# Sliding attention by pairs of heads on two token tiles, and the first pair of each feed-forward written out

## What is computed

```python
kb, vb = band(k), band(v)                      # key blocks n-1 and n
scores = einsum('bnqhgd,bnkhd->bnhgqk', qb, kb) * (Dh ** -0.5)
scores = where(valid, scores, -inf)            # causal, window of 128
m = maximum(max(scores, axis=-1), sink)
e = exp(scores - m)
denom = sum(e, axis=-1) + exp(sink - m)
out = einsum('bnhgqk,bnkhd->bnqhgd', e / denom, vb)
```

## Time and profile before

| | |
|---|---|
| median of 3 runs | 2503.91 us |
| lowest and highest | 2501.05, 2506.88 us |
| the profiled execution | 2497.86 us |
| its span in the profile | 2495.9 us |
| mean granted clock of TensorE | 0.966 |
| busy in the span | PE 94%, DVE 51%, ACT 31%, POOL 6% |

### The profile page before, as it was taken

How to read it: one execution, slowest core, us unless ns; L and a number is a source line. 1 busy time by engine, 2 the same in 40 slices (tenths; PEclk the granted TensorE clock), 3 DMA queues, 4 the chain that set the end, 5 groups by cost and what they waited for, 6 DMA issues and landing times.

```text
span 2495.9 us, 28634 instructions
## 1 busy us (share of the span) xinstructions
PE 2348.9 (94%) x11659; PEld 1887.8 (76%) x11659; DVE 1281.8 (51%) x1541; ACT 776.6 (31%) x1002; POOL 139.6 (6%) x92
## 2 busy tenths in 40 slices
PE   6999999996899999999987999999988889999998
PEld 5888888865688888787875778888766647788887
DVE  5434445647454345475567454444557763534543
ACT  3312233243233322353236321222333353312211
POOL 2000001103100100020000100000100000000000
PEclk9999999988899999999999999999999899999999
DMA  4333223210032232233320133233221300233221
GB/s 138 101 101 97 89 84 95 85 55 1 26 101 101 84 101 84 84 101 102 93 77 1 52 101 98 87 103 99 74 87 44 92 1 21 99 101 101 87 99 68
DMA packets 192321, 200.54 MB, mean 80 GB/s; under 512 B 6178, under 2 KB 187520, under 8 KB 192226
## 3 DMA queue, kind: packets, MB, share of 16 engines
q1 hardware_dynamic: 192226, 199.22, 25.2%
HBM read 191.93 MB, written 2.10 MB: 78 GB/s over the span
## 4 chain that ended last, share of the span: by engine, by line
PE 83%; DVE 11%; ACT 3%; issue 2%; DMA 1%; SPq 0%; POOL 0%; DVEq 0%; ACTq 0%
PE psum L541 81%; DVE w_lo L258 1%; PE psum L933 1%; DVE sm L1891 1%; DVE free_x L1964 1%; ACT w_hi L250 1%; DVE sm L1962 1%; ACT free_h L1094 1%; PE psum L751 1%; DVE free_x L1462 0%; DVE h_lo L1465 0%; DVE rstd L1480 0%; DVE xg_lo L1462 0%; DVE free_h L1465 0%; DVE buf_b L1462 0%
## 5 line engine op out<-in xcount | busy, mean ns | idle before, releaser
L541 PE MATMUL psum<-xg_lo,w_hi 128*128 128x512 f32 x1568 | 609.8, 391 | 4.0 <-DVE xg_lo L1462 2.7
L541 PE MATMUL psum<-xg_hi,w_hi 128*128 128x512 f32 x1520 | 595.8, 392 | 2.7 <-DVE w_lo L258 2.6
L541 PE MATMUL psum<-xg_hi,w_lo 128*128 128x512 f32 x1520 | 592.6, 390 | 0.0
L250 ACT ACTIVATE w_hi<-w_raw 128x2048 fp32r<-128x2048 f32 (+1 forms) x183 | 348.2, 1903 | 535.5 <-PE psum L541 520.9
L258 DVE TENSOR_TENSOR w_lo<-w_raw,w_hi 128x2048 fp32r<-128x2048 f32 (+1 forms) x183 | 419.1, 2290 | 179.5 <-ACT w_hi L250 179.4
L541 PE MATMUL psum<-h_hi,w_hi 128*128 128x512 f32 x1144 | 453.5, 396 | 4.8 <-DVE w_lo L258 3.0
L541 PE MATMUL psum<-h_lo,w_hi 128*128 128x512 f32 x1144 | 447.7, 391 | 0.0
L541 PE MATMUL psum<-h_hi,w_lo 128*128 128x512 f32 x1144 | 447.5, 391 | 0.0
L541 PEld LDWEIGHTS psum<-xg_lo,w_hi 128*128 128x128 f32 x1568 | 295.5, 189 | 69.7 <-issue 6.5
L541 PEld LDWEIGHTS psum<-xg_hi,w_hi 128*128 128x128 f32 x1520 | 286.3, 188 | 66.6 <-issue 5.7
L541 PEld LDWEIGHTS psum<-xg_hi,w_lo 128*128 128x128 f32 x1520 | 286.2, 188 | 60.0
(11 more groups left out here) (228 smaller groups left out, 2258.9 us busy)
## 6 DMA issues: line engine op xcount, KB each, us to landing
w_raw<-in_mlp_w SPq DMA_DIRECT2D x64, 1024.0 KB, 5.2
w_raw<-in_ffn_w_gate SPq DMA_DIRECT2D x22, 1024.0 KB, 5.3
w_raw<-in_ffn_w_up SPq DMA_DIRECT2D x22, 1024.0 KB, 5.3
w_raw<-in_ffn_w_down SPq DMA_DIRECT2D x16, 1024.0 KB, 5.0
w_raw<-in_diff_w_in SPq DMA_DIRECT2D x12, 1024.0 KB, 5.1
w_raw<-in_w_in SPq DMA_DIRECT2D x9, 1024.0 KB, 5.1
w_raw<-in_dsa_w_in SPq DMA_DIRECT2D x9, 1024.0 KB, 5.1
w_raw<-in_ffn_w_down SPq DMA_DIRECT2D x8, 768.0 KB, 4.3
```

Of the source, the lines that this page charges most:

```text
L250: e.activation(w_hi[:, c % 2, 0:n], w_raw[:, c % 2, 0:n], ACT.Copy).then_inc(sem("hi_done"), 1)
L541: return pe.matmul(out, lhsT, rhs, start=start, stop=stop)
```

## The change

**Sliding attention.** A unit `u` is now a pair of heads (t = u // 2) on two of the four token tiles (0 and 1 for even u, 2 and 3 for odd u). Each head of the pair has one of the two banks, and one product of 512 columns writes the masks of both tiles into a bank (for tiles 2 and 3 the same 256 columns are read twice). Behind both masks come the scores tile by tile, the head in the lower half of the array and the head in the upper half in turn. The values go tile by tile too, the two halves of the output partitions in turn. Transposes, their copies, the exponentials and the normalisation keep shape and count: again eight units of four tiles. Since a unit now has two heads, the sinks are read for both: VectorE keeps them negated, takes the minimum with the negated maximum, and subtracts in one more small instruction, which gives the argument of the small exponential. The wait for a free output bank stands before even units only. The mask constants change places so that 512 columns in a row serve tiles 0 and 1.

**Feed-forwards.** On ScalarE and VectorE the pair j = 0 of the first group of each feed-forward is written out ahead of the loop, which then starts at 1. In this pair ScalarE does `hi` of block c+2 ahead of its first activation; in the squared form VectorE also does `lo` of block c+2 ahead of the first evacuation. In the gated form VectorE's order stays.

```diff
@@ TensorE
-            def a1_scores(h):
-                half, kv = h % 2, h // 4
...
-                for n in range(NT):
-                    dst = bank[2 * (h % 2) + n // 2][:, (n % 2) * 256:(n % 2 + 1) * 256]
-                    mm(dst, ident_bf[:], first_mask if n == 0 else band_mask, True, False)
...
-                        last = mm(dst, q, keys[hs, (n - 1) * P:(n + 1) * P], False, True)
+            def a1_scores(u):
+                t, kv = u // 2, u // 4
+                if u >= 2:
+                    pe.wait_ge(sem("a1_exp"), u - 1)
+                for half in range(2):
+                    dst = bank[2 * (u % 2) + half]
+                    if u % 2 == 0:
+                        mm(dst, ident_bf[:], first_mask, True, False)
+                    else:
+                        mm(dst.rearrange("p (b k) -> p b k", b=2), ident_bf[:],
+                           band_mask.unsqueeze(1).to_broadcast([P, 2, 2 * P]), True, False)
+                for b in range(2):
+                    n = 2 * (u % 2) + b
+                    for half in range(2):
+                        hs = slice(HD * half, HD * half + HD)
+                        keys = ak if half == kv else ak_swap
+                        first = P if n == 0 else 0
+                        last = mm(bank[2 * (u % 2) + half][:, b * 256 + first:(b + 1) * 256],
+                                  aq[hs, t, n * P:(n + 1) * P], keys[hs, (n - 1) * P + first:(n + 1) * P], False, b == 1)
...
-                if t >= 2:
+                if t >= 2 and u % 2 == 0:
                     pe.wait_ge(sem("a1_out"), t - 1)
-                for n in range(NT):
+                for b in range(2):
+                    n = 2 * (u % 2) + b
                     for w in ((1,) if n == 0 else (0, 1)):
...
+                        for half in range(2):
+                            last = mm(bank[6 + t % 2][HD * half:HD * half + HD, n * P:(n + 1) * P],
+                                      av[:, n - 1 + w, kv * HD:(kv + 1) * HD],
+                                      a1_pt(u)[:, 4 * half + 2 * b + w, :], w == 0 or n == 0, w == 1)
@@ ScalarE
+                    def square_pair(j, first=False):
+                        if first:
+                            hi(act, c + 2, j)
+                        for s_ in range(2):
+                            act.wait_ge(sem("hmul"), 2 * j + (h0 + s_ + 1))
+                            a(hidden(p)[0][:, bass.ds(4 * j + 2 * s_, 2), :], buf_d[:], ACT.Copy).then_inc(sem("h_hi_done"), 1)
+                            if s_ or not first:
+                                hi(act, c + 2 + s_, j)
...
-                a(sm[:, so + 12:so + 16], sm[:, so + 4:so + 8], ACT.Exp,
-                  bias=sinks[:, h:h + 1]).then_inc(sem("a1_exp"), 1)
+                a(sm[:, so + 12:so + 16], sm[:, so + 12:so + 16], ACT.Exp).then_inc(sem("a1_exp"), 1)
@@ VectorE
+                    def square_pair(j, first=False):
+                        if first:
+                            lo(dve, c + 2, j)
+                        for s_ in range(2):
+                            evac_scaled(c + s_, buf_b, j)
...
+                            if s_ or not first:
+                                lo(dve, c + 2 + s_, j)
...
-                ts(sm[:, so + 4:so + 8], sm[:, so:so + 4], sinks[:, h:h + 1], -1.0, ALU.max, ALU.mult).then_inc(sem("a1_m"), 1)
+                sink = no_sinks[:, h // 2 * 2:h // 2 * 2 + 2].unsqueeze(2).to_broadcast([P, 2, 2])
+                low = sm[:, so + 4:so + 8].rearrange("p (a b) -> p a b", b=2)
+                link(stt(low, sm[:, so:so + 4].rearrange("p (a b) -> p a b", b=2), -1.0, sink, ALU.mult, ALU.min))
+                tt(sm[:, so + 12:so + 16].rearrange("p (a b) -> p a b", b=2), low, sink, ALU.subtract).then_inc(sem("a1_m"), 1)
```

More of the change, by code:

```diff
@@ L1116, in ffn, with gated_pair @@
                     hcount[0] += tiles // 2
+                    def gated_pair(j, first=False):
+                        if first:
+                            hi(act, c + 2, j)
+                        act.wait_ge(sem("evac"), 2 * j + (c + 1))
+                        a(buf_c[:], buf_a[:], ACT.Silu).then_inc(sem("silu"), 1)
+                        if not first:
+                            hi(act, c + 2, j)
+                        act.wait_ge(sem("hmul"), j + (h0 + 1))
+                        a(hidden(p)[0][:, bass.ds(2 * j, 2), :], buf_d[:], ACT.Copy).then_inc(sem("h_hi_done"), 1)
+                        hi(act, c + 3, j)
@@ new lines, in square_pair @@
+                    def square_pair(j, first=False):
+                        if first:
+                            hi(act, c + 2, j)
+                        for s_ in range(2):
[3 more added lines that the diff above has]
+                                hi(act, c + 2 + s_, j)
+                    pair, n_pairs = (gated_pair, tiles // 2) if gated else (square_pair, tiles // 4)
@@ L1117, in ffn @@
+                    if g == 0:
+                        pair(0, first=True)
                     if gated:
                         scount[0] += tiles // 2
-                        with act.Fori(0, tiles // 2) as j:
-                            act.wait_ge(sem("evac"), 2 * j + (c + 1))
-                            a(buf_c[:], buf_a[:], ACT.Silu).then_inc(sem("silu"), 1)
-                            hi(act, c + 2, j)
-                            act.wait_ge(sem("hmul"), j + (h0 + 1))
-                            a(hidden(p)[0][:, bass.ds(2 * j, 2), :], buf_d[:], ACT.Copy).then_inc(sem("h_hi_done"), 1)
-                            hi(act, c + 3, j)
-                    else:
-                        with act.Fori(0, tiles // 4) as j:
-                            for s_ in range(2):
-                                act.wait_ge(sem("hmul"), 2 * j + (h0 + s_ + 1))
-                                a(hidden(p)[0][:, bass.ds(4 * j + 2 * s_, 2), :], buf_d[:], ACT.Copy).then_inc(sem("h_hi_done"), 1)
-                                hi(act, c + 2 + s_, j)
+                    with act.Fori(1 if g == 0 else 0, n_pairs) as j:
+                        pair(j)
@@ L1543, in ffn @@
+                    with dve.Fori(1 if g == 0 else 0, n_pairs) as j:
+                        pair(j)
                     if before_down and g == 0:
```

102 lines of the change are left out of this document (46 added, 56 removed).

## The result

| | before | after |
|---|---|---|
| median of the runs, us | 2502.48 (2500.85 to 2506.88) | 2476.49 (2476.01 to 2481.79) |
| time of the profiled execution, us | 2497.86 | 2481.79 |
| its span, us | 2495.9 | 2479.7 |
| sliding attention, first mask to the next stage's first product, us | 71.55 | 54.48 |

The ratio of the medians is 0.9898, with a 95% interval of 0.9879 to 0.9917: shorter by 26.0 us, which is 1% and clear of the interval, where 16.5 was forecast. The profiled executions alone stand 16.1 apart.

The account below looks back on a forecast made before the run. TensorE was taken as the bound, 83% of the last-ending chain. Savings of 13.5 us in sliding attention and 3.0 at feed-forward starts, 16.5, took 2497.86 to 2481.4 profiled, plus 6.05 to a 2487 median; range 2480 to 2498.

Parts of the forecast that it names:

- T(0) to T(1): ... Half: 2.4 saved: Sliding attention, first to second unit's transposes: 3.3 us at full clock or 4.9 at half, against 7.26; 2.4 saved.
- T(1) to T(2): ... The middle: 2.7: Sliding attention, second to third unit's transposes: 4.3 us saved at full clock or 1.05 at half, 2.7 taken.
- give-back of 0.9: Sliding attention: 0.9 us given back for one of the third, fifth or seventh units' transposes running at half clock.
- S(2) ... 8.6 or 10.1: Sliding attention, up to the first transposes, third unit's scores included: 8.6 or 10.1 us against 12.62; 2.5 saved.
- T(6) to T(7): V(5) is in the chain: 0.7 saved, or 1.0 lost at half clock: Sliding attention, seventh to eighth unit's transposes: the sixth unit's values saving 0.7 us, or 1.0 lost at half clock.
- So the wait goes entirely: 1.34 + 1.69 = 3.03: Starts of the two squared feed-forwards: TensorE's wait for the third weight block's split vanishes, 3.03 us saved.
- In the gated ones ... nothing: Starts of the two gated feed-forwards: no wait there to remove, so nothing saved.
- The median of the runs lies 6.05 above it, so 2487: Whole kernel: 6.05 us between profiled execution and median added to the forecast profiled time of 2481.4, giving 2487.
- A: Rival, sliding attention: the clock stays full, 23.0 us saved in all, 2481; chance 0.10.
- B: Rival, sliding attention: the clock stays half, 7.3 us saved in all, 2497; sign granted clock below 0.65; chance 0.15.
- C: Rival, sliding attention: halves in turn do not overlap, only 3.0 us saved, 2501; chance 0.04.
- D: Rival, sliding attention: halves do not overlap and the stage stays at half clock, 13.5 us lost, 3.0 won, 2514; chance 0.03.

Follow-up runs that it names:

- run with the filled wait: Changed kernel plus 16 unread 512-column mask products in TensorE's wait between the scores of units 1 and 2; 2479.65 us, ratio 0.9914 to the kernel before.
- attention-only kernel: Kernel before with the changed kernel's sliding attention and its own old feed-forward loops; 2488.99 us, ratio 0.9943 to the kernel before.
- scores experiment: Changed kernel with each head's mask and two score matmuls ahead of the other head's, halves not in turn; 2491.5 us, ratio 0.9948 to the kernel before.
- first session: The original measurement of the changed kernel against the kernel before; 2476.49 us, ratio 0.9898.
- second session: The changed kernel, unchanged, timed again beside the kernel before; 2481.23 us, ratio 0.9916.
- repetitions: Both kernels run again unchanged: the kernel before 2502.06 us, ratio 1.0002; the changed kernel 2481.23 us, ratio 0.9916.
- the low half later: Changed kernel with VectorE's low half of a head pair's output and next-stage keys behind the next normalisation; 2469.09 us, ratio 0.986 to the kernel before.
- values-in-blocks run: Changed kernel with the values of one head first, then those of the other; 2479.07 us, ratio 0.9895 to the kernel before.
- kernel before with the later low half: Kernel before with VectorE's low half of a head pair's output and next-stage keys behind the next normalisation; 2488.84 us, ratio 0.9957.

## Why the prediction was wrong

**The mechanisms held in kind.** The halves overlap (eight in 1.14 instead of 2.3), the unit's scores (1.64, and 1.46 with the shorter first tile, forecast 1.5) and values (1.03 and 0.81, forecast 1.0 and 0.8) have their price. T(2) to T(3) and T(4) to T(5) kept their length and only turned TensorE's work into waiting (saved 0.10 and 0.09, forecast 0). T(3) to T(4) gave 4.0 of 3.8. The weight split's waits went. The short intervals came out at 3.33, 3.29 and 3.23, near the floor of 3.3 that was set for VectorE. But no T waits at their ends: they are TensorE's own T, V and S. VectorE's floor shows once, in the run with the filled wait, where T(1) waits for it 3.07 us behind T(0): 0.2 under the forecast.

**"T(0) to T(1): ... Half: 2.4 saved" and "T(1) to T(2): ... The middle: 2.7"** are the terms that were mis-sized in the stage. They measured 3.93 and 4.46, which is what the prediction's full clock gives (4.0 and 4.3). "TensorE has just idled over 3 us, so I take half" was right for T(0) alone (1.86), and T(1), 3.3 us later, is back at 1.10. I had carried a fall of the clock over two more intervals, because the earlier trace rows shows one that lasts from 528 to 545. There, though, the work behind the wait was one half of the array at a time. With both halves at work the fall ended in the same interval. That the halves are the reason is a reading, not shown. The risk was not unreal: the attention-only kernel, with the same instructions, has its half clock at T(3) to T(4), which took 5.93 there instead of 3.23. The scores experiment shows the other side: with the halves one after the other again, half clock goes from 17.1 to 37.5 us, though TensorE idles less in that stage (2.0 and 3.2 ahead of T(3) and T(5) instead of 3.15 and 4.36). These two terms are 3.3 us of the 3.6 that the stage gave beyond the forecast; of the rest, the first interval and T(5) to T(6) gave 0.75 and 0.3 more, T(6) to T(7) 0.7 less once the give-back of 0.9 is counted there, the tail 0.5 less.

**"S(2) ... 8.6 or 10.1"** for the first interval: 9.38, between the two, since only T(0) and the scores ahead of it were slow.

**"T(6) to T(7): V(5) is in the chain: 0.7 saved, or 1.0 lost at half clock"**: 0.88 lost, all of it T(6), at 1.97 instead of 1.09, which is the 0.9 given back for one T. The 0.7 of V(5) did not come either, as it took its first part at half clock too:

```profile
564.11 1.74 PE L541 MATMUL psum<-free_x,arena 128*64 128x128 f32 x16
```

16 in 1.74, as long as 14 in one half at full clock before. The chain behind it through VectorE kept its length; the stall of 2.30 us was there before the change as well.

**"So the wait goes entirely: 1.34 + 1.69 = 3.03"** was right in kind, small by 0.4 us in each of the two places (1.73 and 2.08); where these 0.4 us come from stays open. **"In the gated ones ... nothing"** was wrong by 0.35 and 0.34 in the trace, and perhaps by more in the medians.

**"The median of the runs lies 6.05 above it, so 2487"** is the step that put the time outside the range. It took the distance between one execution and the median of three as a constant that carries over to the changed kernel. There the profiled execution lies above the median instead, by 5.3 us in the first session and 0.6 in the second. With the stage and the starts as they were measured (21.6 saved instead of 16.5), the same step would still have given 2482.3, inside the range. The profiled execution of before was a favourable one: its stage was 71.5 us where three others of the same attention code had 75.7 to 75.9, and of 61 later executions of that kernel, on three chips, two are as short as its 2497.86. Four runs also put its median at 2502.48 instead of 2503.91. In the second session the gain by medians, 21.3, is 4.8 above the forecast's 16.5, close to the 5.0 that its two sums were small by. The further 4.7 us of the first session stay open.

Taken against the profiled execution, the forecast was 2481.4 and the measured one is 2481.79. That agreement is chance: the stage and the starts gave 5 us more than forecast, and falls of the clock elsewhere took as much. From weight split to weight split the changed kernel loses 1.6 and 1.5 us ahead of the sliding attention, 0.7 in the linear attention, 1.6 around 990 us and 4.2 in the top-k attention, and gains 1.2, 1.6 and 1.0 where the kernel before has falls around 1140, 1810 and 1930 us: 5.8 us lost in all. By medians the difference is 21 to 26 us, by the profiled executions 16.1.

**The rivals.** A, full clock, has the short intervals right, and its time (2481) is that of the second session. But the granted clock was 0.84, two T took 1.97, and the stage's 17.1 lies between the forecast's 13.5 and A's 20. B, that the clock stays half, did not come in the changed kernel: less work on TensorE and more idle time went with a higher granted clock, 0.84 against 0.76 and, in the repetitions, 0.84 against 0.71. It is not ruled out as a part: the attention-only kernel, with the same instructions, stood at 0.71, its stage 5 us longer, still above the 0.65 that was to be B's sign. The Trainium skill ("TensorE: Matmul & The Clock Gate", Part 1) says that activity releases the throttle. The trace agrees where a T follows a wait of 6.59 us (1.97), and the filled wait agrees too (1.09 behind 3.63 us of filling). It is not borne out by T(3), at 1.09 behind a wait of 3.15, and it gives no ground to sum that over a stage. C and D fell with the first row of scores: the halves do overlap.

## What to carry over

Where matmuls use half of the array, put two independent ones with opposite halves side by side. In rows the second was free here: eight instructions in turn took 1.14 us, four of one half 1.13. In columns it nearly was: 16 in turn took 1.03 us, where 14 in one half took 1.68, which by estimate makes 0.96 for eight. Behind such a gain the stage's length is set by the order on the other engines: the next 12 us here lay in two steps, the low half and the keys, that made VectorE wait for ScalarE ahead of work that TensorE needed, and the cost was visible as waits in the earlier trace rows before anything was changed. When a few microseconds in 2500 are at stake, take several profiled executions of the unchanged kernel before adding the difference between trace and median as a constant.

## What the runs showed of the hardware beyond that

The granted clock falls at different places in the same code. In the top-k attention the changed kernel has, over 400 us behind the last changed instruction ahead of it, this window:

```profile
1866.00:1884.00 18.00, 15.65 (x47) 8.79 (x47) 4.09 (x6) 4.73 (x9) 0.00 (x0) 0.53 0.00 0
```

and these rows, each of four instructions that use 64 rows, half of the array:

```profile
1864.18 1.61 PE L541 MATMUL psum<-arena 64*128 64x512 f32 x4 [1.18 <-ACT buf_c L1103]
...
1869.64 2.56 PE L541 MATMUL psum<-arena 64*128 64x512 f32 x4 [1.18 <-ACT buf_c L1103]
```

The two groups of the kernel before, with the same waits:

```profile
1882.14 1.61 PE L541 MATMUL psum<-arena 64*128 64x512 f32 x4 [1.17 <-ACT buf_c L1094]
1886.51 1.61 PE L541 MATMUL psum<-arena 64*128 64x512 f32 x4 [1.17 <-ACT buf_c L1094]
```

Same instructions, same waits of 1.2 us, 1.61 or 2.56 long: 4.2 us over the whole stretch. The changed kernel run again has the fall in the same place; with the low half later it begins one group later (1.61 in the second group, 2.56 in the third). TensorE was busy 15.65 of the 18 us there. What sets the place of such a fall could not be settled by these runs. In the values-in-blocks run the same window stands at 0.72.

The clock also falls where TensorE has no gap at all. A window of the profiled execution of before, inside dense weight products:

```profile
290.00:300.00 10.00, 10.00 (x44) 7.55 (x43) 5.33 (x9) 4.65 (x4) 0.00 (x0) 1.00 0.25 83
```

and the same window in the repetition of that kernel:

```profile
290.00:300.00 10.00, 10.00 (x39) 7.44 (x38) 4.48 (x7) 4.65 (x4) 0.00 (x0) 0.87 0.29 99
```

TensorE is busy for all 10 us in both, at 1.00 and at 0.87. Ahead of the sliding attention there are two such places in the repetition and in the changed kernel, costing 1.6 and 1.5 us, and none in the first execution of before. The first of them stands in all profiled executions but two, that one and the one of the kernel before with the later low half. They are a part of what one execution can differ from another without any change of code.
